# Hybrid decode step in float32: attention values as stationary operand, probabilities normalised before they are turned, the sampled tile's steps between the levels of the triangular solves

## What is computed

```python
def mixer_layer(x, ple, pos, past_k, past_v, dn_s, dn_buf, rw_s, rw_prev, lp):
    proj = rmsnorm(x, lp['norm_g']) @ lp['w_in']
    qkv_a, z_a, beta_raw, alpha_raw, f_b, z_b, qkv_c, z_c, gate_raw = split(proj)
    o_a, dn_s_new = gated_delta_chunked(q_a, k_a, v_a, g_a, beta, dn_s)   # branch a: 4 heads of 128
    o_a = rmsnorm(o_a, lp['onorm_a']) * silu(z_a)
    y_b, rw_s_new = rwkv7_scan(r_h, logw, k_h, v_h, -kk, kk * a_h, rw_s)  # branch b: 8 heads of 64
    o_b = (groupnorm(y_b) + bonus) * silu(z_b)
    q_c, k_c = (rope_partial(rmsnorm(t), pos) for t in (q_c, k_c))        # branch c: 8 heads of 64
    p = softmax(where(mask, q_c @ k_all.T * D_C ** -0.5, -inf))
    o_c = (p @ v_all) * silu(z_c)
    up = einsum('blnc,ncd->blnd', stack([o_a, o_b, o_c]), lp['w_branch'])
    x = x + sum(sigmoid(gate_raw + b_gate) * up) @ lp['w_out']
    return x + sigmoid(x @ lp['w_pg'] + b_pg) * (ple @ lp['w_ple'])
```

## Time and profile before

| | us |
|---|---|
| median of 3 runs | 1184.14 (1183.62 to 1186.87) |
| the profiled execution, whole | 1179.26 |
| its span, first to last instruction | 1177.0 |
| TensorE busy | 1139.6 (97% of the span) |
| VectorE busy | 570.0 (48%) |
| ScalarE busy | 323.7 (27%) |
| GpSimd busy | 131.7 (11%) |
| mean granted TensorE clock | 0.975 of full speed |

### The profile page before, as it was taken

One profiled execution on the slowest core, in us unless ns is written; L12 is line 12 of the kernel. 1 busy time (PEld: TensorE's weight loads), 2 busy tenths in 40 slices (PEclk: granted clock), 3 DMA queues, 4 the chain that ended last, 5 costly groups with the idle time before them and its releaser, 6 DMA issues.

```text
span 1177.0 us, 20908 instructions
## 1 busy us (share of the span) xinstructions
PE 1139.6 (97%) x8148; PEld 871.2 (74%) x8148; DVE 570.0 (48%) x1251; ACT 323.7 (27%) x718; POOL 131.7 (11%) x215
## 2 busy tenths in 40 slices
PE   7999999999899999999999999999998999999998
PEld 5777877778678687777767778777775877777776
DVE  4576466755735605221245764756566454161212
ACT  2243213312413243300123332233133132433001
POOL 0212041020111100000001120501102011000000
PEclk9999999999959999999999999999997899999999
DMA  6833136413303775364237322543232067453621
GB/s 217 250 108 114 55 109 198 125 39 97 86 2 117 202 221 176 90 212 146 74 113 209 113 77 89 163 142 91 72 98 50 19 210 199 153 157 108 218 83 41
DMA packets 168654, 148.44 MB, mean 126 GB/s; under 512 B 41705, under 2 KB 157007, under 8 KB 168365
## 3 DMA queue, kind: packets, MB, share of 16 engines
q1 hardware_dynamic: 164167, 136.65, 39.4%
q0 software_dynamic: 2848, 7.79, 1.9%
q10 hardware_dynamic: 1541, 2.66, 0.7%
HBM read 135.42 MB, written 11.07 MB: 124 GB/s over the span
## 4 chain that ended last, share of the span: by engine, by line
PE 89%; DVE 4%; ACT 2%; SPq 2%; DMA 2%; issue 1%; POOL 0%; ACTq 0%; DVEq 0%; POOLq 0%
PE psum L1150 63%; PE psum L1075 4%; PE psum L1343 2%; PE psum L1326 2%; PE psum L1200 1%; PE psum L1457 1%; PE psum L1718 1%; PE psum L1554 1%; PE psum L1564 1%; PE psum L1338 1%; PE psum L1323 1%; ACT arena L1785 1%; PE psum L1697 1%; SPq L976 1%; PE psum L1578 1%
## 5 line engine op out<-in xcount | busy, mean ns | idle before, releaser
L1150 PE MATMUL psum<-x_b,ring 128*128 128x288 f32 x1296 | 343.0, 415 | 1.7 <-DMA ring<-in_w_in 1.7
L1150 PE MATMUL psum<-x_a,ring 128*128 128x288 f32 x1296 | 340.2, 413 | 0.5 <-DVE x_a L2246 0.5
L1150 PEld LDWEIGHTS psum<-x_b,ring 128*128 128x128 f32 x1296 | 241.2, 192 | 71.3 <-issue 8.2
L1150 PEld LDWEIGHTS psum<-x_a,ring 128*128 128x128 f32 x1296 | 239.3, 191 | 68.9 <-issue 8.7
L1785 ACT ACTIVATE arena<-psum 128x512 f32<-128x512 f32 (+5 forms) x150 | 67.2, 472 | 182.9 <-PE psum L1075 68.9
L1150 PE MATMUL psum<-z,ring 128*128 128x288 f32 x384 | 99.7, 409 | 0.0
L1150 PEld LDWEIGHTS psum<-z,ring 128*128 128x128 f32 x384 | 70.6, 190 | 17.9 <-issue 0.7
L1150 PE MATMUL psum<-merged,ring 128*128 128x288 f32 x256 | 62.4, 406 | 0.0
L1785 ACT ACTIVATE arena<-arena 128x256 f32<-128x256 f32 (+9 forms) x102 | 44.5, 464 | 64.1 <-DVE arena L2833 28.7
L1075 PE MATMUL psum<-consts,arena 128*128 128x128 f32 (+2 forms) x362 | 53.2, 279 | 6.2 <-DMA arena<-in_x_prompt 4.6
L1150 PEld LDWEIGHTS psum<-merged,ring 128*128 128x128 f32 x256 | 48.6, 190 | 13.4
(11 more groups left out here) (404 smaller groups left out, 1430.1 us busy)
## 6 DMA issues: line engine op xcount, KB each, us to landing
ring<-in_w_in SPq DMA_DIRECT2D x72, 1024.0 KB, 5.3
ring<-in_w_branch SPq DMA_DIRECT2D x24, 512.0 KB, 3.6
arena<-in_cache_k SPq DMA_DIRECT2D x32, 256.0 KB, 3.1
arena<-in_cache_v SPq DMA_DIRECT2D x32, 256.0 KB, 3.2
ring<-in_w_out SPq DMA_DIRECT2D x8, 1024.0 KB, 6.3
ring<-in_w_pg SPq DMA_DIRECT2D x8, 1024.0 KB, 5.1
arena<-in_state_dn SPq DMA_DIRECT2D x8, 512.0 KB, 8.0
out_dn_sample<-arena POOLq DMA_DIRECT2D x8, 512.0 KB, 6.5
```

The lines of the kernel that those rows point to most:

```text
L1150: ins = mm(out[:, 0:NTOK], lhs, rhs(k), **flags)
```

## The change

- The sampled tile's steps move. as_scale to as_o and a_norm2 of tile 2 stand between lev_y and lev of the six levels of u = 0; bs_scale to bs_y, b_norm1 and b_norm2 of tile 2 in the same way in u = 1 and 2; the rest of their norms and as_out, bs_out stand among the prompt tiles' outputs. For that they get other PSUM banks and buffers, and waits tied to given steps.
- bs_out goes head pair by head pair (two calls, one bank); b_hist comes before 43 pieces instead of behind them; c_sq, c_rms, c_turn come ahead of c_fetch_k. FILL is new: 674 fillers as before, 21 pieces in the third solve instead of 3; 33 pieces between c_turn and c_rope(1), 11 between that and c_nat(1).
- c_prob: VectorE multiplies the probabilities by 0.5 and the inverse row sum before TensorE turns them; TensorE waits for that. c_pv: CVN is stationary (64 columns), CPT moves (128 columns), two heads in two column halves; the result is already turned, and VectorE multiplies it straight into Z. c_out and CON's part in it go.
- c_past: GpSimd copies the new keys behind the cached ones (CKT has 288 columns now), one run of 16 matmuls instead of two; c_spv: uniform tiles of 128x32, rows of zeros set by GpSimd. ScalarE's c_nat waits for that (c_qx).

```diff
-    def both_tiles(u):
+    def both_tiles(u, beside={}):
...
             add("lev_y", u, k)
+            for s in beside.get(k, ()):
+                add(*s)
             add("lev", u, k)
...
-    both_tiles(0)
+    both_tiles(0, {1: [("as_scale",)], 2: [("as_pairs",)], 3: [("as_sq",), ("as_inv",)], 4: [("as_s0",), ("as_w",)],
+                   5: [("as_u",), ("as_o",)], 6: [("a_norm2", 2)]})
...
-        both_tiles(1 + g)
+        add("bs_nat", g)
+        both_tiles(1 + g, {1: [("bs_scale", g)], 2: [("bs_pairs", g)], 3: [("bs_in", g), ("bs_sq", g)],
+                           4: [("bs_s0", g), ("bs_inv", g), ("bs_w", g)], 5: [("bs_u", g), ("bs_y", g)],
+                           6: [("b_norm1", g, 2), ("b_norm2", g, 2)]})
...
             def bs_out(l, g, pr):
...
-                for pr in range(2):
-                    for hh in range(2):
-                        r, o = rows_of(half_of(hh, pr)), rows_of(hh)
-                        ins = mm(M[pr][o, :], BN[r, pr, 0, o], BX[r, pr, :, :], start=True, stop=True)
+                for hh in range(2):
+                    r, o = rows_of(half_of(hh, pr)), rows_of(hh)
+                    ins = mm(M[0][o, :], BSKN[r, pr, o], BX[r, pr, :, :], start=True, stop=True)
...
             def c_prob(l, t, g):
-                pe.wait_ge(S.sem("c_e"), S.count("c_e"))
-                pe.wait_ge(S.sem("c_done"), S.count("c_done"))
+                pe.wait_ge(S.sem("c_sp"), S.count("c_sp"))
+                pe.wait_ge(S.sem("c_sdone"), S.count("c_sdone"))
...
             def c_pv(l, t, g):
-                for hd in range(4):
+                for pr in range(2):
                     for st in range(t + 1):
-                        ins = mm(M[4][:, 64 * hd:64 * hd + 64], CPT[:, st, hd, :], CVN[:, st, 64 * (4 * g + hd):64 * (4 * g + hd) + 64],
-                                 start=st == 0, stop=st == t)
+                        for hh in range(2):
+                            hd = 2 * pr + hh
+                            ins = mm(M[4][rows_of(hh), 128 * pr:128 * pr + 128], CVN[:, st, 64 * (4 * g + hd):64 * (4 * g + hd) + 64],
+                                     CPT[:, st, hd, :], start=st == 0, stop=st == t, skip_group_check=True)
...
-            def c_out(l, t):
-                for m in range(4):
-                    ins = tr(M[2][:, 128 * m:128 * m + 128], CON[:, 128 * m:128 * m + 128])
...
                 link(dve.reciprocal(CMX[:, 2, :], CMX[:, 1, :]))
+                for hd in range(4):
+                    p = CP[:, hd, 0:128 * (t + 1)]
+                    ins = ts(p, p, CMX[:, 2, hd:hd + 1], 0.5, MUL, MUL)
...
-                tt(CON[:, 256 * g:256 * g + 256].rearrange("p (h n) -> p h n", h=4),
-                      M[4][:, 0:256].rearrange("p (h n) -> p h n", h=4), bc(CMX[:, 2, :], 2, [128, 4, 64]), MUL).then_inc(S.sem("c_os"), 1)
+                z = Z[:, 2, 2 * g:2 * g + 2, tok(t)]
+                tt(z, M[4][:, 0:256].rearrange("p (q n) -> p q n", q=2), z, MUL).then_inc(S.sem("c_done"), 1)
...
+                pool.memset(CVN[:, 2, :], 0.0)
+                pool.memset(CPTS[:, 2, :], 0.0)
+                new = QC[:, 4:8, SEQ:NTOK].unsqueeze(1).to_broadcast([128, 4, 4, NS])
+                pool.tensor_copy(CKT[:, :, :, SEQ:NTOK], new).then_inc(S.sem("c_qx"), 1)
```

More of the change, by code:

```diff
@@ L199 @@
     "ba_neg": {"a_rows": (1, None)},
-    "c_done": {"c_out": (1, None)},
+    "c_done": {"c_pv": (1, None)},
     "c_e": {"c_prob": (1, None), "c_sprob": (1, None)},
@@ L204 @@
     "c_o": {"c_pv": (1, None)},
-    "c_os": {"c_pv": (1, None)},
-    "c_ot": {"c_out": (1, None), "c_sout": (1, None)},
+    "c_ot": {"c_sout": (1, None)},
     "c_pt": {"c_prob": (1, None)},
@@ L744, in program @@
         CKN, CVN = part(3, W), part(3, W)
-        CKT = part(4, 4, 256)
+        CKT = part(4, 4, NTOK)
         SQ = arena[:, 0:8 * NTOK].rearrange("p (i a n) -> p i a n", i=2, a=4)
@@ L750, in program @@
         CPT = part(2, 4, 128)
-        CMX = part(3, 4)
-        top[0] = CQX_AT
+        CMX = SMP[:, 0, 0:12].rearrange("p (a b) -> p a b", a=3)
+        top[0] = CQX_AT + 256
         CQX = part(4, NSEQ, 32)
@@ L1408, in a_norm5 @@
             def a_norm5(l, t):
-                pe.wait_ge(S.sem("a_nat"), S.count("a_nat"))
-                pe.wait_ge(S.sem("a_w"), S.count("a_w"))
                 pe.wait_ge(S.sem("out_normed"), S.count("out_normed"))
-                for h in range(1 if t == 2 else 4):
-                    ins = tr(v4(M[4], 128)[:, h, :], a_out(t)[:, h, :])
+                if t == 2:
+                    pe.wait_ge(S.sem("tri_up"), S.count("tri_up"))
+                    ins = tr(M[0][:, 0:128], ASO)
+                else:
+                    pe.wait_ge(S.sem("a_w"), S.count("a_w"))
+                    for h in range(4):
+                        ins = tr(v4(M[4], 128)[:, h, :], a_out(t)[:, h, :])
                 ins.then_inc(S.sem("out_t"), 1)
@@ L1747, in _ @@
                       b_fin=b_fin, b_norm5=b_norm5, c_rms=c_rms, c_rope=c_rope, c_nat=c_nat, c_score=c_score,
-                      c_prob=c_prob, c_pv=c_pv, c_out=c_out, c_keys=c_keys, c_past=c_past, c_sprob=c_sprob, c_spv=c_spv, c_sout=c_sout, y_out=y_out)
+                      c_prob=c_prob, c_pv=c_pv, c_keys=c_keys, c_past=c_past, c_sprob=c_sprob, c_spv=c_spv, c_sout=c_sout, y_out=y_out)
             for i, st in enumerate(order):
@@ L2901, in _ @@
                       bs_scale=bs_scale, bs_pairs=bs_pairs, bs_in=bs_in, bs_sq=bs_sq, bs_w=bs_w, bs_u=bs_u, bs_y=bs_y, bs_out=bs_out,
-                      c_turn=c_turn, c_rope=c_rope, c_score=c_score, c_prob=c_prob, c_pv=c_pv, c_out=c_out, c_sprob=c_sprob, c_sout=c_sout,
+                      c_turn=c_turn, c_rope=c_rope, c_score=c_score, c_prob=c_prob, c_pv=c_pv, c_sprob=c_sprob, c_sout=c_sout,
                       y_out=y_out)
```

241 lines of the change are left out of this document (111 added, 130 removed), and 12 rows, old and new, of the table FILL.

## The result

| | kernel before | changed kernel |
|---|---|---|
| median of the runs | 1185.24 us (4 runs) | 1176.99 us (1175.01 to 1179.00, 4 runs) |
| ratio, 95% interval | | 0.993 (0.9907 to 0.9954) |
| a second time, 5 rounds | 1181.63 us | 1177.47 us, 0.9941 (0.9919 to 0.9964) |
| profiled execution, span | 1179.26, 1177.0 us | 1179.00, 1177.1 us |
| mean granted clock | 0.975 | 0.994 |

The change is faster, by 0.6 to 0.7%; 1154.1 us was forecast, with a range of 1139 to 1172. The forecast's gain of 30 us came to 8. The changed kernel's profiled execution is the slowest of its four and that of before the fastest of its own, so the two traces are compared part by part and not by their spans.

The account below looks back on a forecast made before the run. TensorE was taken to bound the kernel, with its instructions, waits and lower-clock losses. The terms summed to -30.1 us, 1149.2 from the profiled 1179.3, or 1154.1 us on the runs' median basis; forecast's own range 1144 to 1163, wider range 1139 to 1172.

Parts of the forecast that it names:

- The third solve, -29.7: Third solve of both layers and the stretch behind it: feeding projections saves TensorE's idling and half clock, -29.7 us.
- The rotary swap, +3.5: Ahead of c_rope(1): 33 pieces fall short of the swap chain by 0.8 and 2.7 us, +3.5 (0 to 6).
- The multiplications of c_prob, +3.0: Attention: VectorE's normalising before the transposes adds 8.4 us in 8 blocks, mostly hidden by fill, +3.0 (0 to 8).
- bs_out, in +2.2: Sampled tile's outputs: half of the old waits kept for as_out(1) and pairwise bs_out, together +2.2 us (0 to 4).
- c_pv, -3.7: Attention: overlapping column halves halve c_pv, -5.3, shape changes add 1.6; net -3.7 us (-3.7 to +1.6).
- c_out, -1.75: Attention: c_out's 16 transposes go, -1.75 us.
- c_past and c_spv: Attention: one run of 288 columns in c_past and a saved shape change in c_spv, together -0.8 us (-2 to 0).
- Steps between the levels, +3.0: Six level stages: moved sampled steps queue on VectorE ahead of the levels, 0.5 us a stage, +3.0 (0 to 9).
- The waits where the steps had stood (-5.8): Old places of the sampled steps: TensorE's waits at as_out, bs_out, sampled norm and lora weights go, -5.8 us.
- the rival on the slow side: Levels: VectorE bounds them and the kernel gets slower, 1199 us at 1.5 us a gap; chance 0.07.
- new waits twice to three times as large: Attention, swap and levels: one chain each is longer than seen, +12 us, 1166 us; chance 0.14.

Follow-up runs that it names:

- e20: Changed kernel with bs_store(1) moved behind c_fetch_k(1), the rotary swap's DMAs issued by ScalarE, and bs_out for both head pairs in one step: 1158.85 us, ratio 0.9808.
- e3: Kernel before with only FILL changed: 18 projection pieces moved into the third solve from three steps just behind it; 1171.48 us, ratio 0.9899.
- e19: Changed kernel with bs_store(1) moved from ahead of b_norm3(1,1) to just behind c_fetch_k(1), the swap still in SyncE's queue: 1163.65 us, ratio 0.9848.
- e1: Changed kernel with the four DMAs of the rotary swap issued by ScalarE instead of SyncE: 1164.68 us, ratio 0.9836.
- e6: Changed kernel without the four multiplications of the probabilities in c_prob, TensorE waiting for ScalarE's exponentials again: 1171.21 us, ratio 0.989.
- e7: Kernel before with the change's attention alone put in (multiplications ahead of the transposes, values stationary, no c_out): 1202.20 us, ratio 1.0128.
- e8: As e1, with 9 of the 22 pieces ahead of c_rope(1) moved ahead of the four c_prob: 1175.84 us, ratio 0.9929.

## Why the prediction was wrong

- **The third solve, -29.7: right in mechanism, and near in size.** Clock 1.00, fed: all seen. The stage from the third solve to c_past(0) fell by only 7.5 us in the two layers together, but with the stores and bs_out put right (e20) it is 15.2 and 13.1 us shorter than before, 28.3 in all (the stage holds smaller terms too). What "the projections that stood there before move behind" left out is that they had covered something: e3 shows a price of 15 us of waits for its own 18 pieces. What it was in the changed kernel, apart from the swap, isn't shown. Changes of tile shape were left out too: 298 between successive records before, 330 after, at about 0.1 us each between 64x64 and 128x128, some 3 us; I had priced them for c_pv alone.
- **The rotary swap, +3.5: the step that failed most.** It took the 16.2 and 18.1 us of the earlier trace rows for the chain's length in the new order and counted pieces against it. Their first part is the time from a DMA's issue to its landing (7.9 us before, 13.6 now), and the change moves 16 stores ahead, so that 4 MB of weights go out in a burst just before the swap. The waits were 11.3 us, and the clock stood at half for 6.8 us in and behind each, some 5 of them with TensorE at work. Half of that is lost, so an estimate is 11.3 + 2 x 2.5 = 16 us for 3.5; by the ledger, e19's stage is 14.8 us shorter in the two layers. e1 and e19 took 10 to 13 us off, one with the swap ahead of the weights, the other with the weights spread out. The order of SyncE's issues, read from the timeline around 380 us before predicting, would have shown it.
- **The multiplications of c_prob, +3.0: 7.0**, most of it at least on the path (e6). "Most is hidden" rested on the number of pieces ahead; e7 and e8 show that it is not the number that decides. Three pieces after the last product, the phase of three of the four blocks in the changed kernel, still left 0.7 to 1.5 us.
- **bs_out, in +2.2:** it took waits into account and not the quadrants: 4.2 us more for the same matmuls, and 1.1 more wait.
- **c_pv, -3.7: right.** The column halves overlap: L1667's 96 records were 11.9 us of busy time, L1665's are 7.0; start to start, shape changes in it, 10.6 and 6.4, so -4.1. The Trainium skill's advice in "TensorEngine Tiling (Array Packing)", Performance Considerations, to swap and tile by columns at a free dimension of 64, is borne out, at a factor of 1.6. The changes of shape cost 0.2 us for the two of a block, as forecast: the record into 128x64 starts 0.34 us after a projection's instead of 0.24, and the one out of it 0.20 us after the last pair instead of 0.10. The rule on mode switching in the Trainium skill ("TensorEngine Tiling (Array Packing)", Key Properties) is borne out too. **c_out, -1.75**: right. c_past and c_spv came to -0.9 for -0.8.
- **Steps between the levels, +3.0:** waits there are 1.3 us for L2487, 0.3 for L1322 on ScalarE and 0.6 for L1521, a sampled step. VectorE is busy 16.8 of 24.3 us in a solve (0.7 us a level more, where 1.3 was forecast) and does not bound it; the rival on the slow side fell. The waits where the steps had stood (-5.8): 1.6 for the sampled norm is left of 2.1, as_out's are gone.
- **b_lora to solve 2**, 1.8 us a layer longer, was in no term. 0.7 of it are small waits; the rest was not taken apart.

Of the rivals, "new waits twice to three times as large" came nearest: it named attention and swap, at +12; the outcome is +23. Of these 23 us, e20 takes back 15 to 18 by mending the swap and bs_out; 4 more are the multiplications'.

## What to carry to other kernels

A step moved for one engine moves in every queue: list what SyncE issues around the new place, with its issue time (16 small stores were 8.8 us), and ask what now goes out behind it. Filler work covers a round trip only if the other engines' parts of the filler, its evictions, don't stand in their queues ahead of the step that is waited for; count from the last eviction, not the number of fillers. And a filler that is moved to a starved stage can be paid for where it stood (e3).

## What the runs showed of the hardware

- The 288 KB swap took 13.6 us from issue to landing behind a burst of 4 MB of weights, and 9.7 behind the same weights issued one by one (e19). From ScalarE's own queue it took at most 9.6 when it went out ahead of the weights (e1) and 10.9 beside them (e20). Which part of this is the queue and which the share of the DMA engines no run separates.
- In TensorE's wait of 6.0 us, with other matmuls on both sides, the granted clock fell to 0.50 for 6.8 us (401.5 to 409.0 shows 0.54). In e8, with waits up to 2.5 us, there are four spells of 3.4 us at 0.50; in e1, where no wait behind the kernel's start is over 1.7 us, there is none before the end.
- 64x64 matmuls of 512 columns took 0.25 us a record start to start with two quadrants in use, 0.13 with four.
